# High and low parts in place of plain 32-bit matmuls: the convolution norm's two sums and the pointwise projection of stage three

## The chip, the cores and the metric

One Trainium2 chip, one of its cores. The metric is the device time of one launch in microseconds (us), median of the runs. The engines named here: TensorE (PE; PEld is its weight load), VectorE (DVE), ScalarE (ACT), GpSimd (POOL), and SyncE (SP), which issues the loads.

## The reference, cut to what matters

Three transformer-like stages on 256 tokens of width 1024, all in float32. Each stage is a mixer (attention) followed by a gated MLP. The change lies in the third stage's mixer. Beside an attention of 8 heads it has a convolution branch and a pooling branch, and all three are concatenated before the output projection:

```
def layer_norm(x, g, b):
    mu = jnp.mean(xf, axis=-1, keepdims=True)
    var = jnp.mean(jnp.square(xf - mu), axis=-1, keepdims=True)
    y = (xf - mu) * lax.rsqrt(var + EPS)
    return y * g + b

def conformer_conv(u, dw_w, dw_b, ln_g, ln_b, pw_w):   # 256 channels
    a, b = jnp.split(u, 2, axis=-1)
    h = a * jax.nn.sigmoid(b)
    h = causal_depthwise_conv(h, dw_w) + dw_b
    h = layer_norm(h, ln_g, ln_b)
    h = jax.nn.silu(h)
    return h @ pw_w

mix = jnp.concatenate([att, conv, pool], axis=-1)
x = x + mix @ w_out
```

## The kernel before, in words

The channels lie on the partitions and the 256 tokens along the free dimension, so an activation of 1024 channels is eight tiles of 128x256. Weights are streamed from memory in chunks of up to 128x1024 through a ring of six buffers. Every projection is computed from high and low parts: ScalarE copies a chunk to the format `float32r` (`w_hi`, L415, "split high"), VectorE subtracts that from the chunk (`w_lo`, L423, "split low"), and TensorE adds three products, high x high, low x high and high x low. Such a matmul takes one instruction record of TensorE. A matmul on plain float32 operands is recorded as two.

Each engine has its own instruction queue, written out by hand, and works through it in order; an instruction that waits for a semaphore holds up everything behind it in that queue. The order is given by Python functions, one for each engine and stage. In the third stage's mixer they are `att_c_pe`, `att_c_act` and `att_c_dve`. All three loop over n = 0 to 15, the 16 chunks of the q, k, v weights: four head pairs p, four chunks each (o = n mod 4). At each n TensorE runs the 12 matmuls of chunk n (L714 to L716, 384 columns each, 392 for the first pair), ScalarE first splits chunk n+4 high, and VectorE first splits chunk n+3 low. The other steps are hung onto values of n. In the list below, "pair 0" is the first head pair.

- Attention chain of pair p, over about two pairs of chunks: squares (L1024) and v (L1049 to L1052) on ScalarE at the next pair's o = 0; sums (L1188) on VectorE; logarithm and exponential (L1035, L1038) on ScalarE at o = 1; normalised q and k (L1202) on VectorE; transposes (L793) on TensorE at o = 3; q and k copies (L1124, L1217); scores (L860, L806) on TensorE; mask and row maximum (L1262, L1269) on VectorE; exponential `exp_act` (L1132) on ScalarE; division (L1274, L1278) on VectorE; transposes of the probabilities `prob_t_pe` (L949) on TensorE; their copy `prob_t_act` (L1139) on ScalarE. The scores of pair p+1 go to the same PSUM banks as those transposes, so `score_c_pe` waits for `prob_t_act` of pair p (semaphore `aC_ptr`).
- Forget gates of the heads, between them: L1146, L1151 to L1175, and `decay_pe` (L831) after chunk 8, which `decay_act` (L839) on ScalarE waits for ahead of its v copies.
- Convolution branch: depthwise convolution `conv_pe` (L2157) after chunks 1 and 2; its sum over taps and over the two channel tiles on VectorE (L2184, L2187); `ln_sum_pe` (L2191), a matmul with an all-ones matrix that adds over the channels, after chunk 3; centring and squaring on VectorE (L2196 to L2202); `ln_var_pe` (L2206) after chunk 4; reciprocal root on ScalarE (L2210, L2213) at n = 5; scaling (L2218) on VectorE and `ln_silu_act` on ScalarE at n = 6: it loads the table with Silu (L2221), runs two Silu (L2224), and loads the table with logarithm and exponential back (L2226); the pointwise projection `pw_pe` (L2257) after chunk 13; its high and low parts for the output projection at n = 14 (L2263, L2268).
- Pooling branch: a matmul after chunk 5 (L2234), parts at n = 6 (L2242, L2248).

After the loop the output projection (L1363 to L1365) runs with the last pairs' steps between its matmuls, then the MLP.

Of the kernel before, what the change touches and what calls it, by code (L numbers as in the profile page):

```python
# [197 lines left out]
def build(nc, x_d, xa_d, stream_d, par_d, con_d, taps_d, out_d):  # L198
# [10 lines left out]
    def sem(name):  # L209
# [61 lines left out]
    decay_rows = sb("decay_rows", [P, 3 * P], F32R)  # L271
    fg_all = sb("fg_all", [P, 2, 2, 2, LO_ROW], F32R)
    fg_hi, fg_lo = [fg_all[:, n, :, :, 0:HEADS_C] for n in range(2)]
    cv_shift = [[cv_s0[:, c * W_SHIFT:(c + 1) * W_SHIFT] for c in range(SHIFTS)],
                [v_tok[c][:, TOK:TOK + W_SHIFT] for c in range(3)] + [prob_t[:, 0, 2, 0:W_SHIFT]]]
    W_PL = POOL_PAD + TOK
# [112 lines left out]
    ln_dve = sem("ln_dve")  # L389
    ln_act = sem("ln_act")  # L390
    side_lo = sem("side_lo")
    pool_pe = sem("pool_pe")
    pool_hi = sem("pool_hi")

# [1285 lines left out]
    def att_c_pe(eng):  # L1680
        for n in range(N_C):
            p, o = divmod(n, UCH)
            unit_chunk_pe(eng, 2, n)
            if n == 1:
                conv_pe(eng, 0)
            if n == 2:
                conv_pe(eng, 1)
            if n == 3:
                ln_sum_pe(eng)
            if n == 4:  # L1690
                ln_var_pe(eng)
            if o == 0 and p >= 3:
                prob_t_pe(eng, 2, p - 3, 0)
            if o == 1 and p >= 2:
                score_c_pe(eng, p - 2)
            if o == 1 and p >= 3:
                pv_pe(eng, 2, p - 3)
            if n == 5:
                pool_mm_pe(eng)
            if n == 8:  # L1700
                decay_pe(eng)
            if n == N_C - 3:
                pw_pe(eng)
            if o == 3 and p >= 1:
                if p == 1:
                    eng.wait_ge(side_lo, 2)
                if p == 3:
                    eng.wait_ge(side_lo, 4)
                qkt_pe(eng, 2, p - 1)
        p = PAIRS_C - 1  # L1710
        out_first(eng, 2, 0, UPPER)
        prob_t_pe(eng, 2, p - 2, 0)
        out_first(eng, 2, 1, UPPER)
        score_c_pe(eng, p - 1)
        pv_quarters_pe(eng, 2, p - 2)
# [12 lines left out]
        out_first(eng, 2, 5, LOWER)  # L1728
        pv_quarters_pe(eng, 2, p)
        out_first(eng, 2, 6, LOWER)  # L1730
        out_second(eng, 2, 4, UPPER)
        out_first(eng, 2, 7, LOWER)
        out_second(eng, 2, 5, UPPER)
        out_second(eng, 2, 6, UPPER)
        out_second(eng, 2, 7, UPPER)

    def att_c_act(eng):
        for n in range(N_C):
            p, o = divmod(n, UCH)
            split_hi(eng, C_QKV + n + AHEAD_HI)  # L1740
            if o == 0 and p >= 1:
                square_act(eng, 2, p - 1, TOK)
                if p == 1:
                    forget_raw_act(eng)
                if n == 8:
                    decay_act(eng)
                v_act(eng, 2, p - 1)
            if o == 0 and p >= 3:
                prob_t_act(eng, 2, p - 3, 0)
            if n == 5:  # L1750
                ln_rsqrt_act(eng)
            if n == 7:
                forget_hi_act(eng)
            if o == 1 and p >= 1:
                norm_act(eng, 2, p - 1, 0, 4)
            if n == 6:
                pool_mix_act(eng)
                forget_log_act(eng)
                ln_silu_act(eng)
            if o == 2 and p >= 3:  # L1760
                mix_act(eng, 2, p - 3)
            if n == N_C - 2:
                conv_mix_act(eng)
            if o == 2 and p >= 2:
                exp_act(eng, 2, p - 2, 0)
                exp_act(eng, 2, p - 2, 1)
            if o == 3 and p >= 1:
                q_act(eng, 2, p - 1)
        p = PAIRS_C - 1
        square_act(eng, 2, p, TOK)  # L1770
        v_act(eng, 2, p)
        prob_t_act(eng, 2, p - 2, 0)
        norm_act(eng, 2, p, 0, 4)
        split_hi(eng, C_OUT + 4)
        exp_act(eng, 2, p - 1, 0)
        exp_act(eng, 2, p - 1, 1)
        mix_sum_act(eng, 2, p - 2)
        split_hi(eng, C_OUT + 5)
        q_act(eng, 2, p)
        prob_t_act(eng, 2, p - 1, 0)  # L1780
        split_hi(eng, C_OUT + 6)
        exp_act(eng, 2, p, 0)
        exp_act(eng, 2, p, 1)
        mix_sum_act(eng, 2, p - 1)
        split_hi(eng, C_OUT + 7)
        split_hi(eng, C_FFN)
        prob_t_act(eng, 2, p, 0)
        mix_sum_act(eng, 2, p)
        split_hi(eng, C_FFN + 1)
        split_hi(eng, C_FFN + 2)  # L1790
        end_act(eng, 5)
        split_hi(eng, C_FFN + 3)

    def att_c_dve(eng):
        for n in range(N_C):
# [14 lines left out]
            if n == 8:  # L1810
                decay_dve(eng)
            if n == 4:
                ln_center_dve(eng)
            if o == 0 and p >= 1:
                sums_dve(eng, 2, p - 1, 0, 4)
            if o == 1 and p >= 1:
                norm_dve(eng, 2, p - 1, p - 1, 0, 0, 4)
                if p == 1:
                    forget_bias_dve(eng)
            if n == 6:  # L1820
                ln_scale_dve(eng)
                pool_mix_dve(eng)
            if o == 1 and p >= 2:
                mask_dve(eng, 2, p - 2, 0)
            if o == 2 and p >= 3:
# [218 lines left out]
    def pre_act_f(eng):  # L2044

        for n in range(N_PRE):
            split_hi(eng, C_PRE + n + AHEAD_HI)
            if n == 2:
                rows_act(eng, 4)
                cols_act(eng, 2)  # L2050
                nc.scalar.activation(tri[:], con[:, CON_TRI:CON_TRI + 3 * P], ACT.Copy).then_inc(tri_in, 1)
            if n in (3, 5):
                t = n // 2 - 1
# [127 lines left out]
    def conv_out_dve(eng, t):  # L2181
# [3 lines left out]
        if t == 1:  # L2185
            eng.wait_ge(conv_acc, 2)
            nc.vector.tensor_tensor(cv_e[0], cv_acc[0], cv_acc[1], ALU.add).then_inc(conv_acc, 1)  # L2187

    def ln_sum_pe(eng):
        eng.wait_ge(conv_acc, 3)  # L2190
        nc.tensor.matmul(bank(LN_BANK), con[:, CON_ONES:CON_ONES + P], cv_e[0], start=True, stop=True).then_inc(ln_pe, 1)  # L2191

    def ln_center_dve(eng):
        eng.wait_ge(ln_pe, 1)
# [7 lines left out]
        nc.vector.tensor_tensor(cv_e[0], cv_e[0], cv_e[1], ALU.add).then_inc(ln_sq, 1)  # L2202

    def ln_var_pe(eng):
        eng.wait_ge(ln_sq, 3)
        nc.tensor.matmul(bank(LN_BANK, TOK), con[:, CON_ONES:CON_ONES + P], cv_e[0], start=True, stop=True).then_inc(ln_pe, 1)  # L2206

    def ln_rsqrt_act(eng):
        eng.wait_ge(ln_pe, 2)
# [40 lines left out]

    def pw_pe(eng):
        eng.wait_ge(att[2].qe, 2)
        eng.wait_ge(ln_act, 4)
        for o in range(2):
            for t in range(2):
                w = PAR_PW + t * 2 * P + o * P
                last = nc.tensor.matmul(bank(PW_BANK, o * TOK), par[:, w:w + P], cv_a[t], start=(t == 0), stop=(t == 1))  # L2257
        last.then_inc(ln_pe, 1)

    def conv_mix_act(eng):  # L2260
# [327 lines left out]
```

## Time and profile before

| | |
|---|---|
| Time, median of 3 runs | 1024.39 us (1024.37 to 1024.44) |
| Profiled execution, first to last instruction (span) | 1023.2 us |
| What lies around the span | 1.2 us (1024.39 less 1023.2) |
| TensorE busy | 1018.9 us, 8026 matmul records |
| VectorE / ScalarE / GpSimd busy | 880.5 / 687.1 / 349.1 us |
| Granted TensorE clock | 1.000 of full |
| Third stage's mixer, chunks 0 to 15 of q, k, v | about 760.3 to 810.0 us of the span |

The profiled execution has no separate device time in the profile; its span is what the table gives. The ends of matmuls are modelled and overlap (a record of 256 columns lasts 0.28 us where the next one starts 0.11 us later), so for TensorE the starts of the records tell what an operation costs, and its waits show best in the weight loads (PEld). The same holds on ScalarE and VectorE to a lesser degree: the next instruction starts some 0.08 to 0.1 us before the record of the one ahead ends, if it does not need its result.

### The profile page before, as it was taken

Reading aid. Unit: us, or ns where it says so; the run is one execution under the profiler, and the core shown is the slowest. Engines: PE = TensorE matmul, PEld = TensorE weight load, DVE = VectorE, ACT = ScalarE, POOL = GpSimd, SP = SyncE. Lnnn points to the kernel's source line nnn. Section 1 sums busy time; section 2 is a strip of 40 time slices with the busy share of each in tenths; the row PEclk is TensorE's granted clock in tenths of the full one; section 3 lists DMA queues with packets and bytes.
Section 4 is the critical chain, followed back from the end, with each engine's and each line's share of the span. In section 5 each row is a group of like instructions: output and inputs, shape, how many; then the busy total and the mean of one; then the engine's idle time right before and its main releaser. Section 6 shows DMA issues by size and latency. Waiting matters only on the chain.

```text
span 1023.2 us, 22239 instructions
## 1 busy us (share of the span) xinstructions
PE 1018.9 (100%) x8026; PEld 960.4 (94%) x8026; DVE 880.5 (86%) x1535; ACT 687.1 (67%) x1267; POOL 349.1 (34%) x370
## 2 busy tenths in 40 slices
PE   9999999999999999999999999999999999999998
PEld 9999999999999999999999999999998999999998
DVE  7977778787799988887888999988897879999886
ACT  7776766766766665677786766656697776665663
POOL 5312221112255533342111556433350025654332
PEclk9999999999999999999999999999999999999999
DMA  9744465556476666526364566666544536666651
GB/s 318 256 152 151 144 186 155 159 175 205 149 236 195 219 188 202 170 94 217 126 192 153 185 206 213 199 194 193 157 123 135 166 125 213 219 206 195 196 163 42
DMA packets 57753, 183.40 MB, mean 179 GB/s; under 512 B 6352, under 2 KB 9680, under 8 KB 57424
## 3 DMA queue, kind: packets, MB, share of 16 engines
q1 hardware_dynamic: 56816, 181.52, 55.8%
q8 instruction: 45, 0.74, 0.3%
q10 hardware_dynamic: 864, 0.92, 0.3%
q14 instruction: 28, 0.23, 0.1%
HBM read 181.36 MB, written 1.05 MB: 178 GB/s over the span
## 4 chain that ended last, share of the span: by engine, by line
PE 99%; DMA 0%; DVE 0%; ACT 0%; DVEq 0%; issue 0%
PE ps L455 23%; PE ps L457 12%; PE ps L714 10%; PE ps L716 10%; PE ps L715 9%; PE ps L1902 6%; PE ps L1903 6%; PE ps L1904 6%; PE ps L1363 2%; PE ps L1365 2%; PE ps L1364 2%; PE ps L640 1%; PE ps L911 1%; PE ps L806 1%; PE ps L949 1%; PE ps L894 1%
## 5 line engine op out<-in xcount | busy, mean ns | idle before, releaser
L423 DVE TENSOR_TENSOR w_lo<-w_raw,w_hi 128x1024 fp32r<-128x1024 f32 (+2 forms) x369 | 441.2, 1213 | 31.9 <-ACT w_hi L415 31.5
L415 ACT ACTIVATE w_hi<-w_raw 128x1024 fp32r<-128x1024 f32 (+2 forms) x369 | 353.5, 972 | 121.7 <-PE ps L457 102.4
L455 PE MATMUL ps<-xg,w_hi 128*128 128x512 f32 x1056 | 362.8, 390 | 0.0
L457 PE MATMUL ps<-xg,w_lo 128*128 128x256 f32 x1056 | 291.5, 276 | 0.0
L455 PEld LDWEIGHTS ps<-xg,w_hi 128*128 128x128 f32 x1056 | 198.2, 188 | 38.7
L2027 POOL TENSOR_TENSOR prob_t<-prob_t,qkT 128x256 f32<-128x256 f32 x63 | 111.1, 1763 | 257.2 <-ACT prob_t L1948 257.2
L457 PEld LDWEIGHTS ps<-xg,w_lo 128*128 128x128 f32 x1056 | 198.2, 188 | 0.1
L714 PE MATMUL ps<-w_hi,xg 128*128 128x384 f32 (+1 forms) x556 | 192.5, 346 | 0.0
L716 PE MATMUL ps<-w_hi,xg 128*128 128x384 f32 (+1 forms) x556 | 187.3, 337 | 0.0
L715 PE MATMUL ps<-w_lo,xg 128*128 128x384 f32 (+1 forms) x556 | 185.7, 334 | 0.0
L1902 PE MATMUL ps<-g_hi,w_hi 128*128 128x256 f32 x528 | 146.0, 276 | 0.0
L1903 PE MATMUL ps<-g_lo,w_hi 128*128 128x256 f32 x528 | 145.9, 276 | 0.0
L1904 PE MATMUL ps<-g_hi,w_lo 128*128 128x256 f32 x528 | 145.8, 276 | 0.0
L2021 POOL TENSOR_TENSOR qkT<-prob,rms_r 128x256 f32<-128x256 f32 x132 | 122.9, 951 | 16.9 <-DVE prob L1962 12.0
L1995 DVE SCALAR_TENSOR_TENSOR qkT<-qkT,par 128x255 f32<-128x255 f32 (+1 forms) x264 | 112.2, 477 | 6.5 <-ACT qkT L1941 6.4
L1941 ACT ACTIVATE qkT<-qkT,par 128x256 f32<-128x256 f32 x132 | 78.0, 598 | 46.2 <-POOL qkT L2021 44.7
L714 PEld LDWEIGHTS ps<-w_hi,xg 128*128 128x128 f32 x556 | 104.2, 187 | 2.7 <-issue 1.7
L716 PEld LDWEIGHTS ps<-w_hi,xg 128*128 128x128 f32 x556 | 104.5, 188 | 0.0
L715 PEld LDWEIGHTS ps<-w_lo,xg 128*128 128x128 f32 x556 | 104.3, 188 | 0.1
L1902 PEld LDWEIGHTS ps<-g_hi,w_hi 128*128 128x128 f32 x528 | 99.1, 188 | 2.6 <-issue 0.2
L1904 PEld LDWEIGHTS ps<-g_hi,w_lo 128*128 128x128 f32 x528 | 99.1, 188 | 0.0
L1903 PEld LDWEIGHTS ps<-g_lo,w_hi 128*128 128x128 f32 x528 | 99.1, 188 | 0.0
(196 smaller groups left out, 1382.0 us busy)
## 6 DMA issues: line engine op xcount, KB each, us to landing
w_raw<-w_stream SPq DMA_DIRECT2D x228, 512.0 KB, 3.8
w_raw<-w_stream SPq DMA_DIRECT2D x137, 384.0 KB, 3.6
w_raw<-w_stream SPq DMA_DIRECT2D x4, 392.0 KB, 3.1
con<-consts SPq DMA_DIRECT2D x1, 1024.0 KB, 6.8
x_all<-x_t SPq DMA_DIRECT2D x4, 256.0 KB, 5.1
conv_taps<-taps SPq DMA_DIRECT2D x1, 1024.0 KB, 7.2
w_raw<-w_stream SPq DMA_DIRECT2D x4, 192.0 KB, 4.5
x_all<-x_a SPq DMA_DIRECT2D x3, 256.0 KB, 5.6
```

Source lines behind the costliest of these rows:

```text
L415: nc.scalar.activation(w_hi[s][:, 0:w], w_raw[s][:, 0:w], ACT.Copy).then_inc(w_hi_done, 1)
L423: nc.vector.tensor_tensor(w_lo(c)[:, 0:w], w_raw[s][:, 0:w], w_hi[s][:, 0:w].bitcast(F32), ALU.subtract).then_inc(w_lo_done, 1)
L455: nc.tensor.matmul(bank(b, 0, 2 * TOK), w_hi[s][:, k * P:(k + 1) * P], xg[:, k, :, :].rearrange("p h t -> p (h t)"), start=(k == 0), stop= ...
L457: last = nc.tensor.matmul(bank(b), w_lo(c)[:, k * P:(k + 1) * P], xg_hi[:, k, :], start=False, stop=(k == KT - 1), skip_group_check=True)
L714: nc.tensor.matmul(out, hi, wh, start=(k == 0), stop=False)
L715: nc.tensor.matmul(out, hi, wl, start=False, stop=False)
L716: last = nc.tensor.matmul(out, lo, wh, start=False, stop=(k == KT - 1))
L1902: nc.tensor.matmul(acc(m), wh, g_hi[b][:], start=first, stop=False, skip_group_check=True)
L1903: nc.tensor.matmul(acc(m), wh, g_lo[b][:], start=False, stop=False, skip_group_check=True)
L1904: last = nc.tensor.matmul(acc(m), wl, g_hi[b][:], start=False, stop=True, skip_group_check=True)
L1995: nc.vector.scalar_tensor_tensor(cv_s[b][s][:, k:TOK], up_s[b][s][:, 0:TOK - k], par_col(f, t, per, i, 4 * s + 2 - k), cv_s[b][s][:, k:TOK ...
L2021: nc.gpsimd.tensor_tensor(up_s[t % 2][s], up_sum[s], rms_r[:], ALU.mult).then_inc(F.up, 1)
```

## The change

The two sums over channels and the pointwise projection no longer use plain float32 operands. Their inputs are split into a `float32r` high part (a copy on ScalarE) and a low part (a subtraction on VectorE), in tiles of `mix_hi` and `mix_lo` that are free until the mixer's results come. The all-ones matrix needs no low part, so each sum is two matmuls; the projection is three matmuls for each of its four old ones. The steps are hung onto later values of n: the sum after chunk 4 (was 3), the variance after chunk 6 (was 4), the Silu with its table loads at n = 9 (was 6), and the scaling on VectorE at n = 8 (was 6).

```
+    ones_r = sb("ones_r", [P, P], F32R)
+    ln_hi, ln_lo = mix_hi[:, 2, :], mix_lo[:, 2, :]
+    pw_hi, pw_lo = [m[:, 0:2, :].rearrange("p k t -> p (k t)") for m in (mix_hi, mix_lo)]
+    silu_hi, silu_lo = mix_hi[:, 2:4, :], mix_lo[:, 2:4, :]
...
 att_c_pe:
-            if n == 3:
+            if n == 4:
                 ln_sum_pe(eng)
-            if n == 4:
+            if n == 6:
                 ln_var_pe(eng)
...
 att_c_act:
-            if n == 5:
-                ln_rsqrt_act(eng)
+            if n == 4:
+                ln_part_act(eng, LN_SUM)
+            if n == 6:
+                ln_part_act(eng, LN_VAR)
...
             if n == 6:
                 pool_mix_act(eng)
                 forget_log_act(eng)
+            if n == 7:
+                ln_rsqrt_act(eng)
+                pw_part_act(eng)
+            if n == 9:
                 ln_silu_act(eng)
+                silu_part_act(eng)
+            if n == N_C - 2:
+                conv_mix_act(eng)
             if o == 2 and p >= 3:
                 mix_act(eng, 2, p - 3)
-            if n == N_C - 2:
-                conv_mix_act(eng)
...
 att_c_dve:
             if n == 4:
+                ln_part_dve(eng, LN_SUM)
+            if n == 5:
                 ln_center_dve(eng)
+            if n == 6:
+                ln_part_dve(eng, LN_VAR)
+            if n == 10:
+                silu_part_dve(eng)
...
             if n == 6:
+                pool_mix_dve(eng)
+            if n == 8:
+                pw_part_dve(eng)
                 ln_scale_dve(eng)
-                pool_mix_dve(eng)
...
 pre_act_f, at n == 2:
+                nc.scalar.activation(ones_r[:], con[:, CON_ONES:CON_ONES + P], ACT.Copy)
...
+    def ln_part_act(eng, no):
+        if no == LN_SUM:
+            eng.wait_ge(conv_acc, 3)
+        else:
+            eng.wait_ge(ln_sq, 3)
+        nc.scalar.activation(ln_hi, cv_e[0], ACT.Copy).then_inc(part_hi, 1)
+
+    def ln_part_dve(eng, no):
+        eng.wait_ge(part_hi, PART0 + no)
+        nc.vector.tensor_tensor(ln_lo, cv_e[0], ln_hi.bitcast(F32), ALU.subtract).then_inc(part_lo, 1)
+
+    def ln_rows_pe(eng, no, out):
+        eng.wait_ge(tri_in, 1)
+        eng.wait_ge(part_lo, PART0 + no)
+        nc.tensor.matmul(out, ones_r[:], ln_hi, start=True, stop=False)
+        nc.tensor.matmul(out, ones_r[:], ln_lo, start=False, stop=True).then_inc(ln_pe, 1)
...
+    def silu_part_act(eng):
+        eng.wait_ge(ln_act, 4)
+        for t in range(2):
+            last = nc.scalar.activation(silu_hi[:, t, :], cv_a[t], ACT.Copy)
+        last.then_inc(part_hi, 1)
...
 pw_pe:
-        eng.wait_ge(ln_act, 4)
+        eng.wait_ge(part_lo, PART0 + SILU)
...
-                last = nc.tensor.matmul(bank(PW_BANK, o * TOK), par[:, w:w + P], cv_a[t], start=(t == 0), stop=(t == 1))
+                nc.tensor.matmul(bank(PW_BANK, o * TOK), pw_hi[:, w:w + P], silu_hi[:, t, :], start=(t == 0), stop=False)
+                nc.tensor.matmul(bank(PW_BANK, o * TOK), pw_hi[:, w:w + P], silu_lo[:, t, :], start=False, stop=False)
+                last = nc.tensor.matmul(bank(PW_BANK, o * TOK), pw_lo[:, w:w + P], silu_hi[:, t, :], start=False, stop=(t == 1))
```

`pw_part_act`, `pw_part_dve` and `silu_part_dve` are the same copy and subtraction for the projection's weights (128x512) and for the low part of the Silu's output (two tiles of 128x256).

Three places show what moves. The first is ScalarE's queue after the v copies of pair 0 (L1052), before the change; L415 is the split of chunk 9, L2210 and L2213 the norm's reciprocal root, L1035 and L1038 the attention's:

```order
L1052 ACTIVATE v_tok<-ps,r_c 128x128 [waits tiles]
L415 ACTIVATE w_hi<-w_raw 128x768 [waits tiles,w_loaded3]
L2210 ACTIVATE ln_x<-ps,con 128x256 [waits ln_pe]
L2213 ACTIVATE ln_x<-ln_x 128x256 [waits ln_act]
L1035 ACTIVATE ln_q<-ss_q,con,r_c 128x4 [waits aC_ss,c_r2]
```

The same place now, where L1058, L421 and L1041 are the old L1052, L415 and L1035, and L2217 is the new high part:

```order
L1058 ACTIVATE v_tok<-ps,r_c 128x128 [waits tiles]
L2217 ACTIVATE mix_hi<-qkT 128x256 [waits conv_acc]
L421 ACTIVATE w_hi<-w_raw 128x768 [waits tiles,w_loaded3]
L1041 ACTIVATE ln_q<-ss_q,con,r_c 128x4 [waits aC_ss,c_r2]
L1041 ACTIVATE ln_q<-ss_q,con,r_c 128x4 [waits aC_ss]
```

The high part of the sum's input stands behind the v copies, which themselves come after chunk 3; the root has gone from here. The second place is TensorE between the last matmuls of chunk 3 and the first of chunk 5, before the change (the ones left out are the 12 of chunk 4):

```order
L716 MATMUL ps<-w_hi,xg 128x392
L2191 MATMUL ps<-qkT,con 128x256 [waits conv_acc]
L714 MATMUL ps<-w_hi,xg 128x384 [waits pre_out,w_lo_done]
...
L716 MATMUL ps<-w_hi,xg 128x384
L2206 MATMUL ps<-qkT,con 128x256 [waits ln_sq]
L714 MATMUL ps<-w_hi,xg 128x384 [waits w_lo_done]
```

And now, with L720 and L722 for L714 and L716, from the end of chunk 3 to the start of chunk 5 (`half_lo` is the semaphore of the low parts):

```order
L722 MATMUL ps<-w_hi,xg 128x392
L720 MATMUL ps<-w_hi,xg 128x384 [waits pre_out,w_lo_done]
...
L722 MATMUL ps<-w_hi,xg 128x384
L2226 MATMUL ps<-mix_hi,ones_r 128x256 [waits half_lo,tri_in]
L2227 MATMUL ps<-mix_lo,ones_r 128x256
L720 MATMUL ps<-w_hi,xg 128x384 [waits w_lo_done]
```

The sum now stands a chunk later, and it waits for VectorE's low part. The third place is ScalarE between the logarithm of pair 1 (n = 9) and the exponential of pair 0 (n = 10), before:

```order
L1035 ACTIVATE ln_q<-ss_q,con,r_c 128x4 [waits aC_ss]
L1038 ACTIVATE r_q<-ln_q 128x8 [waits aC_ln]
L415 ACTIVATE w_hi<-w_raw 128x768 [waits tiles,w_loaded2]
L1132 ACTIVATE prob,ssum<-prob,nmax 128x128 [waits aC_nmax]
L1132 ACTIVATE prob,ssum<-prob,nmax 128x256
```

and now, where L2278 and L2283 are the table loads, L2281 the Silu, L2242 the new high parts, and L1138 the exponential:

```order
L1044 ACTIVATE r_q<-ln_q 128x8 [waits aC_ln]
L2278 ACT_TABLE_LOAD
L2281 ACTIVATE qkT<-qkT,par 128x256 [waits ln_dve] x2
L2283 ACT_TABLE_LOAD
L2242 ACTIVATE mix_hi<-qkT 128x256 [waits ln_act]
L2242 ACTIVATE mix_hi<-qkT 128x256
L421 ACTIVATE w_hi<-w_raw 128x768 [waits tiles,w_loaded2]
L1138 ACTIVATE prob,ssum<-prob,nmax 128x128 [waits aC_nmax]
```

The loads and the Silu now stand ahead of the exponential of pair 0, with the two new copies behind them.

## Rows read from the trace of the kernel before

**Rows 1.** The page: span, and busy time of each engine.

```profile
span 1023.2 us, 22239 instructions
PE 1018.9 (100%) x8026; PEld 960.4 (94%) x8026; DVE 880.5 (86%) x1535; ACT 687.1 (67%) x1267; POOL 349.1 (34%) x370
```

**Rows 2.** Waits of the weight loads, 740 to 1023 us: total, times, longest.

```profile
PEld ps L2206 <- DVE qkT L2202: 0.2, 1, 0.2
```

**Rows 3.** Timeline of PE around the two sums: start, duration, instruction, idle before.

```profile
775.45 0.34 PE L716 MATMUL ps<-w_hi,xg 128*128 128x392 f32 x1
775.63 0.59 PE L2191 MATMUL ps<-qkT,con 128*128 128x256 f32 x2
...
776.24 0.34 PE L715 MATMUL ps<-w_lo,xg 128*128 128x384 f32 x1
...
777.98 0.34 PE L716 MATMUL ps<-w_hi,xg 128*128 128x384 f32 x1
778.20 0.70 PE L2206 MATMUL ps<-qkT,con 128*128 128x256 f32 x2
...
778.91 0.33 PE L715 MATMUL ps<-w_lo,xg 128*128 128x384 f32 x1
```

**Rows 4.** Timeline of PE around the pointwise projection.

```profile
802.08 0.51 PE L860 MATMUL ps<-decay_rows,head_row 128*128 128x384 f32 x2
...
804.03 1.99 PE L2257 MATMUL ps<-qkT,par 128*128 128x256 f32 x8
...
806.04 0.34 PE L715 MATMUL ps<-w_lo,xg 128*128 128x384 f32 x1
```

**Rows 5.** Timeline of PE in the projections ahead: three matmuls of 256 columns.

```profile
754.90 0.28 PE L441 MATMUL ps<-xg,w_hi 128*128 128x256 f32 x1
...
755.24 0.28 PE L441 MATMUL ps<-xg,w_hi 128*128 128x256 f32 x1
```

**Rows 6.** Timeline of ACT after chunk 3.

```profile
777.32 0.37 ACT L1052 ACTIVATE v_tok<-ps,r_c 128x128 f32<-128x128 f32 x1
777.59 0.84 ACT L415 ACTIVATE w_hi<-w_raw 128x768 fp32r<-128x768 f32 x1
```

**Rows 7.** Timeline of ACT: an operation of 256 columns, and the next.

```profile
835.80 0.40 ACT L515 ACTIVATE tokbuf<-x_all 128x256 f32<-128x256 f32 x1
836.11 0.49 ACT L509 ACTIVATE xg<-x_all,par 128x256 fp32r<-128x256 f32 x1
```

**Rows 8.** Timeline of DVE: an operation of 256 columns, and the next.

```profile
777.72 0.42 DVE L2202 TENSOR_TENSOR qkT<-qkT 128x256 f32<-128x256 f32 x1
778.06 0.74 DVE L1188 TENSOR_REDUCE ss_q<-tokbuf 128x4 f32<-128x256 f32 x2
```

**Rows 9.** Timeline of ACT: the Silu and its table loads.

```profile
783.03 0.22 ACT L1161 ACTIVATE fg<-fg 128x16 f32<-128x16 f32 x1
783.26 1.28 ACT L2221 ACT_TABLE_LOAD   x1
784.56 1.10 ACT L2224 ACTIVATE qkT<-qkT,par 128x256 f32<-128x256 f32 x2
785.67 1.28 ACT L2226 ACT_TABLE_LOAD   x1
786.97 0.85 ACT L415 ACTIVATE w_hi<-w_raw 128x768 fp32r<-128x768 f32 x1
```

**Rows 10.** Timeline of ACT from the logarithm of pair 1 to `prob_t_act`.

```profile
792.40 0.21 ACT L1038 ACTIVATE r_q<-ln_q 128x8 f32<-128x8 f32 x1
792.51 0.83 ACT L415 ACTIVATE w_hi<-w_raw 128x768 fp32r<-128x768 f32 x1
794.86 0.40 ACT L1132 ACTIVATE prob<-prob,nmax 128x128 f32<-128x128 f32 x1 [1.52 <-DVE nmax L1269]
...
800.38 0.81 ACT L1139 ACTIVATE prob_t<-ps 128x768 f32<-128x768 f32 x1
```

**Rows 11.** Timeline of PE: the decay matmuls, and the transposes of pair 0's probabilities.

```profile
788.74 0.65 PE L831 MATMUL ps<-tri,fg_all 128*40 128x384 f32 x6
...
799.35 0.82 PE L949 MATMUL ps<-con,prob 128*128 128x128 f32 x6
```

**Rows 12.** Timeline of ACT: waits for TensorE behind the projection.

```profile
806.06 0.66 ACT L2263 ACTIVATE mix_hi<-ps 128x256 fp32r<-128x256 f32 x2 [1.53 <-PE ps L2257]
810.66 0.39 ACT L1124 ACTIVATE qkT<-ps 128x256 f32<-128x256 f32 x1 [1.25 <-PE ps L793]
```

More of the change, by code:

```diff
@@ L391, in build @@
     side_lo = sem("side_lo")
+    part_hi, part_lo, PART0 = half_hi, half_lo, HALVES
+    LN_SUM, LN_VAR, PW_W, SILU = 1, 2, 3, 4
     pool_pe = sem("pool_pe")
@@ L2187, in conv_out_dve, with pw_part_act, pw_part_dve, silu_part_dve @@
             nc.vector.tensor_tensor(cv_e[0], cv_acc[0], cv_acc[1], ALU.add).then_inc(conv_acc, 1)
-    def ln_sum_pe(eng):
-        eng.wait_ge(conv_acc, 3)
-        nc.tensor.matmul(bank(LN_BANK), con[:, CON_ONES:CON_ONES + P], cv_e[0], start=True, stop=True).then_inc(ln_pe, 1)
+    def ln_part_act(eng, no):
[12 more added lines that the diff above has]
+        nc.tensor.matmul(out, ones_r[:], ln_lo, start=False, stop=True).then_inc(ln_pe, 1)
+    def ln_sum_pe(eng):
+        ln_rows_pe(eng, LN_SUM, bank(LN_BANK))
+    def pw_part_act(eng):
+        nc.scalar.activation(pw_hi, par[:, PAR_PW:PAR_PW + 4 * P], ACT.Copy).then_inc(part_hi, 1)
+    def pw_part_dve(eng):
+        eng.wait_ge(part_hi, PART0 + PW_W)
+        nc.vector.tensor_tensor(pw_lo, par[:, PAR_PW:PAR_PW + 4 * P], pw_hi.bitcast(F32), ALU.subtract).then_inc(part_lo, 1)
+    def silu_part_act(eng):
[3 more added lines that the diff above has]
+        last.then_inc(part_hi, 1)
+    def silu_part_dve(eng):
+        eng.wait_ge(part_hi, PART0 + SILU)
+        for t in range(2):
+            last = nc.vector.tensor_tensor(silu_lo[:, t, :], cv_a[t], silu_hi[:, t, :].bitcast(F32), ALU.subtract)
+        last.then_inc(part_lo, 1)
     def ln_center_dve(eng):
@@ L2204, in ln_var_pe @@
     def ln_var_pe(eng):
-        eng.wait_ge(ln_sq, 3)
-        nc.tensor.matmul(bank(LN_BANK, TOK), con[:, CON_ONES:CON_ONES + P], cv_e[0], start=True, stop=True).then_inc(ln_pe, 1)
+        ln_rows_pe(eng, LN_VAR, bank(LN_BANK, TOK))
     def ln_rsqrt_act(eng):
@@ L2252, in pw_pe @@
         eng.wait_ge(att[2].qe, 2)
-        eng.wait_ge(ln_act, 4)
+        eng.wait_ge(part_lo, PART0 + SILU)
         for o in range(2):
             for t in range(2):
-                w = PAR_PW + t * 2 * P + o * P
-                last = nc.tensor.matmul(bank(PW_BANK, o * TOK), par[:, w:w + P], cv_a[t], start=(t == 0), stop=(t == 1))
+                w = t * 2 * P + o * P
+                nc.tensor.matmul(bank(PW_BANK, o * TOK), pw_hi[:, w:w + P], silu_hi[:, t, :], start=(t == 0), stop=False)
+                nc.tensor.matmul(bank(PW_BANK, o * TOK), pw_hi[:, w:w + P], silu_lo[:, t, :], start=False, stop=False)
+                last = nc.tensor.matmul(bank(PW_BANK, o * TOK), pw_lo[:, w:w + P], silu_hi[:, t, :], start=False, stop=(t == 1))
         last.then_inc(ln_pe, 1)
```

## The prediction

> **What bounds the kernel now.** I read the page first: TensorE is busy for 1018.9 of 1023.2 us [rows 1]. Then the waits of its weight loads, because the ends of its matmuls are modelled: from 740 us to the end there is one wait for another engine, 0.2 us at the variance matmul, for VectorE [rows 2]. So TensorE's queue is the time. Work taken out of it is a gain at once, and every new wait in it is a loss at once, with nothing behind it to give it back. The reader has to keep two sums apart: what the matmuls cost by the distance of their starts, and when ScalarE and VectorE are ready for the waits that now stand at other places. For those I read the timelines of the three engines from 775 to 811 us.
>
> **The matmuls.** From the last L716 of chunk 3 to the L715 of chunk 4 are 0.79 us (775.45 to 776.24), around one plain 32-bit matmul [rows 3]. Ten steps later, 777.98 less 776.24, gives 0.174 us for each of the projection's matmuls, so two steps without the sum would be 0.35, and the sum costs 0.44. The same around the variance: 778.91 less 777.98 is 0.93, less 0.35 is 0.58, of which 0.10 is the restart after its wait (778.20 to 778.91 is 0.71, against 0.61 from 775.63 to 776.24 without a wait) and some 0.04 the wait. The four matmuls of the pointwise projection and the change back take 2.01 us, 804.03 to 806.04 [rows 4].
> The new ones have the shape and the format of L441 to L443: three of them in 0.34 us, so 0.114 each [rows 5]. Each sum becomes 2 x 0.114 = 0.23, the projection 12 x 0.114 + 0.17 = 1.54. TensorE's own work falls by 0.21 + 0.35 + 0.47 = 1.03 us. I take the format's price as certain to 0.1 us: reading the parts from the mixer's tiles is what the output projection does too.
>
> **The first new wait: the sum after chunk 4.** Its high part stands on ScalarE behind the v copies. Those end at a time that the change does not touch: L1052 starts at 777.32 and the next instruction at 777.59 [rows 6]. The copy takes 0.40 us [rows 7], to 777.99. VectorE has been free since its split and answers 0.04 later, 0.42 for the subtraction [rows 8], to 778.45; TensorE's weight load follows 0.06 after such an end (777.72 + 0.42 = 778.14 to 778.20 [rows 3, 8]), and with the restart of 0.10 the first matmul counts from 778.61. TensorE, without the old sum, ends chunk 4 at 775.63 + 12 x 0.174 = 777.72. The wait is 0.89 us. What waits behind it is all of TensorE's queue. On VectorE the subtraction stands ahead of pair 0's sums and of the split of chunk 8, which TensorE needs four chunks later.
> The variance follows the same way: centring comes after the split on VectorE, some 1.9 us of it, and the low part is ready at about 784.1, where TensorE ends chunk 6 at about 784.2. I count it as hidden, by 0.1 us; if the cover is gone it costs what it is late, plus 0.16 of restart. Together to this point: 0.89 + 0.23 + 0.23 - 0.44 - 0.58 = +0.33 us.
>
> **The second: Silu and table loads in front of the exponential of pair 0.** `decay_pe` starts 0.33 later than 788.74 [rows 11], and ScalarE, which waits for it, is late by the same. Without Silu at n = 6 it reaches that wait early, and the time saved there is lost in waiting for TensorE. At n = 9 the block goes in behind L1038: the load starts when that is over (783.03 + 0.22 against 783.26 [rows 9]), 0.11 later than the next instruction does now; then from load to load 2.41 (783.26 to 785.67), 1.30 for the second load, and two copies of 0.31 each (835.80 to 836.11 [rows 7]): 0.11 + 2.41 + 1.30 + 0.62 = 4.44 us. Against it stands the idle time that ScalarE has ahead of the exponential: it could begin at 792.51 + 0.74 (the distance of such a split is the 0.83 of its record less 0.09) = 793.25 and begins at 794.86 [rows 10], 1.61 us. So the exponential is late by 0.33 + 4.44 - 1.61 = 3.16.
> From there to `prob_t_act` of pair 0, at 800.38, ScalarE has no idle time now [rows 10], so the 3.16 arrive there whole. The scores of pair 1 wait for that copy: it now ends at 801.19, with 0.06 + 0.10 of restart 801.35, and TensorE comes at 802.08 [rows 4]. The slack is 0.73. TensorE will start those scores 3.16 - 0.73 = 2.43 us late. The transposes at L949, 799.35 [rows 11], wait first, by about 1.1 us, since the division needs the exponential; this is inside the 2.43 and not added to it, and so is the 0.33 of before.
> The projection then gives its 0.47 back: +1.96 at chunk 14. After it ScalarE has two waits for TensorE now, 1.53 and 1.25 us [rows 12], in which its remaining lateness over TensorE (3.16 against 1.96, and 0.3 for the mix copy that now stands behind the projection's) is gone. From there everything moves by the same amount to the end.
>
> **Edits that I cost at nothing.** The copy of the ones (128x128, at about 753 us), the high and low parts of the projection's weights (128x512) and the scaling at n = 8 stand where ScalarE or VectorE wait for TensorE soon after. The Silu needs the scaling, which I put 1.7 us before it; that is the cover, and each us beyond it would be one of time. No DMA is added or moved; SP's queue waits for low splits that are needed some ten us later.
>
> **A rule against rows.** The loads last 1.28 us, and the Silu starts 1.30 after the load does [rows 9]. The Trainium skill, "ScalarE: Activation LUTs", section "What ACT_TABLE_LOAD costs", puts a drain of about 1.38 us beside the load, about 2.66 us for a switch. By that rule two switches would cost some 2.7 us more than the rows show, and the sum would be near 1029; the rows here hold no such drain but for the 0.11 above, and I go by them.
>
> **The sum.** -1.03 (matmuls) + 0.89 (first wait) + 2.10 (the waits at the transposes and scores, 2.43 less 0.33) = +1.96 us. The profiled span would go from 1023.2 to 1025.1, and with the 1.2 us around it the time from 1024.39 to 1026.3. What a measurement here can tell from no change is 0.2%, 2.05 us. The forecast lies just inside.
> The spread of its terms: restart of TensorE 0.06 to 0.25 in place of 0.16, twice; copies on ScalarE 0.31 to 0.40; how much of the 0.33 reaches ScalarE, 0 to 0.33; slack 0.5 to 0.9. Together 1025.6 to 1027.0.
>
> **Rivals.**
> 1. The Silu block is absorbed. ScalarE gets 3.7 us freed at n = 6, and if it carried that forward, the exponential would be in time. Then only the first wait counts: +0.33 - 0.47 = -0.14, 1024.2. For it: the total of work hardly grows. Against it: ScalarE must wait for `decay_pe` in between, so it can't be early after 789 us.
> 2. All waits hidden, the plain gain: -1.03, 1023.4. It needs the low part of the sum before 777.66. Against it: the v copies alone end later.
> 3. Slower than can be overlooked: the Silu waits for VectorE's scaling. There the subtraction of 128x512 and the scaling come behind the decay's low part and pair 1's sums. It decides once VectorE is more than 1.7 us later than I put it; a further split's worth (some 0.9 us) beyond that gives +2.9, 1027.3. For it: VectorE waits for ScalarE's decay copy first. Against it: I find nothing to fill the 1.7.
> 4. The drain of the rule above is real at this place: +4.7, 1029.1.
> 5. The format doesn't give one pass here: 16 matmuls at the old price of about 0.43 instead of 0.114 would be some +5, 1031. Against it: all projections of this kernel, same kind of tiles.
>
> **How the numbers follow.** Forecast 0.70; rival 1: 0.12; rival 2: 0.05; rival 3: 0.10; rivals 4 and 5: 0.03 together. Over 0.2% slower starts at 1026.44: of the forecast's own 0.70 I put 0.28 above it and 0.42 below, with rivals 3 to 5 that is 0.41 slower. Faster by over 0.2% would be under 1022.34, beyond even rival 2: 0.01. Rest 0.58. The predicted time is the forecast's, 1026.3. The range leaves out rival 2, half of rival 1 and the top: 1024.4 to 1027.4; the forecast's own is 1025.6 to 1027.0.
>
> **What would show it.** In the profile after: the waits of TensorE's weight loads list three new ones, at the first sum for VectorE (about 0.8 us), at the transposes of pair 0 for VectorE (about 1.1), at the scores of pair 1 for ScalarE (about 1); each of the new matmuls starts 0.11 us after the one ahead; the exponential of pair 0 starts near 798 with no idle time before it; and from chunk 14 on all starts lie 1.9 to 2.0 us later. The prediction is wrong if TensorE reaches the scores of pair 1 without waiting, if the variance waits for more than 0.3 us, if a Silu waits for VectorE, or if the lateness of chunk 14 is not that of the end.

## The result, and the profile after

| | before | after |
| --- | --- | --- |
| Median of 11 runs | 1024.44 us (1024.20 to 1024.73) | 1027.03 us (1026.55 to 1027.65) |
| Ratio to before | | 1.0026, 95% interval 1.0018 to 1.0034 |
| Span of the profiled run | 1023.2 us | 1025.1 us |

The changed kernel is slower by 2.6 us, 0.26%; forecast were +1.9 us, range 1024.4 to 1027.4. The median falls on the slower side of the bound of 0.2% that the forecast stood just inside of, but the interval reaches from 0.18% to 0.34% and so holds that bound.

The page after, span and busy times, against [rows 1]:

```profile
span 1025.1 us, 22260 instructions
PE 1018.4 (99%) x8030; PEld 958.7 (94%) x8030; DVE 881.8 (86%) x1540; ACT 688.9 (67%) x1273; POOL 348.7 (34%) x370
```

TensorE's busy time falls by 0.5 us while the span grows by 1.9: the time went into waits. The span of before is of one execution that was long in its first part: in every run that has both figures the time is 1.8 us more than the span (1.76 to 1.88), so a time of 1024.4 goes with a span of 1022.6, and the typical span grew by 2.6. The weight loads' waits after, 740 us to the end (total, times, longest), against [rows 2]:

```profile
PEld ps L955 <- DVE prob L1284: 1.2, 1, 1.2
PEld ps L2226 <- issue: 1.0, 1, 1.0
PEld ps L866 <- ACT prob_t L1145: 0.9, 1, 0.9
...
PEld ps L1923 <- issue: 0.3, 1, 0.3
...
PEld ps L2314 <- issue: 0.2, 1, 0.2
```

Three are at the places forecast: the transposes of pair 0 (L955, before L949), the first sum (L2226), the scores of pair 1 (L866, before L860). The second says "issue", but PE's own timeline names the releaser, the low part's subtraction L2221:

```profile
778.21 0.35 PE L2226 MATMUL ps<-mix_hi,ones_r 128*128 128x256 f32 x1 [0.72 <-DVE mix_lo L2221]
778.40 0.28 PE L2227 MATMUL ps<-mix_lo,ones_r 128*128 128x256 f32 x1
...
783.91 0.28 PE L2226 MATMUL ps<-mix_hi,ones_r 128*128 128x256 f32 x1
784.03 0.28 PE L2227 MATMUL ps<-mix_lo,ones_r 128*128 128x256 f32 x1
...
800.39 0.87 PE L955 MATMUL ps<-con,prob 128*128 128x128 f32 x6 [0.87 <-DVE prob L1284]
...
803.94 0.61 PE L866 MATMUL ps<-decay_rows,head_row 128*128 128x384 f32 x2 [0.59 <-ACT prob_t L1145]
...
805.99 0.39 PE L2314 MATMUL ps<-mix_hi 128*128 128x256 f32 x1
806.21 0.28 PE L2315 MATMUL ps<-mix_lo,mix_hi 128*128 128x256 f32 x1
806.33 0.28 PE L2316 MATMUL ps<-mix_hi,mix_lo 128*128 128x256 f32 x1
...
807.53 0.34 PE L720 MATMUL ps<-w_hi,xg 128*128 128x384 f32 x1
807.71 0.34 PE L721 MATMUL ps<-w_lo,xg 128*128 128x384 f32 x1
```

Rows 3, 4 and 11 of before have their counterparts here. The variance (783.91) has no wait, as forecast. ScalarE's timeline shows the block of the Silus behind the logarithm of pair 1, against [rows 9, 10]:

```profile
789.45 0.48 ACT L845 ACTIVATE decay_rows<-ps 40x384 fp32r<-40x384 f32 x1 [0.91 <-PE ps L837]
...
792.41 0.21 ACT L1044 ACTIVATE r_q<-ln_q 128x8 f32<-128x8 f32 x1
792.63 1.28 ACT L2278 ACT_TABLE_LOAD   x1
793.93 1.09 ACT L2281 ACTIVATE qkT<-qkT,par 128x256 f32<-128x256 f32 x2
795.04 1.28 ACT L2283 ACT_TABLE_LOAD   x1
796.33 0.72 ACT L2242 ACTIVATE mix_hi<-qkT 128x256 fp32r<-128x256 f32 x2
796.96 0.83 ACT L421 ACTIVATE w_hi<-w_raw 128x768 fp32r<-128x768 f32 x1
797.70 0.38 ACT L1138 ACTIVATE prob<-prob,nmax 128x128 f32<-128x128 f32 x1
...
803.08 0.80 ACT L1145 ACTIVATE prob_t<-ps 128x768 f32<-128x768 f32 x1
```

The exponential starts at 797.70 with no idle time before it; it was 794.86 after 1.52 of idle time. The copy that the scores wait for starts at 803.08 in place of 800.38.

**How two traces are laid on each other.** Executions differ by some tenths at the first loads and between 741 and 755 us, whatever the kernel. So each instruction of TensorE was matched with the same one of before, and the difference of their starts is given relative to that at 755 us, ahead of everything in dispute but the copy of the ones (752.75 in the changed kernel). That copy shows no cost: between 741 and 755 us the kernels fall into two groups, about 0.37 us apart, and both groups hold kernels with it and without it (after and before; after_again and order_only). Columns are times in the trace of before (us); 779 is behind the two sums of before, 799.5 the transposes, 802.3 the scores, 806.1 behind the projection, 1016 and 1019 the last MLP.

| Kernel | 779.0 | 784.5 | 799.5 | 802.3 | 806.1 | 1016 | 1019 |
| --- | --- | --- | --- | --- | --- | --- | --- |
| after | +0.16 | +0.38 | +1.47 | +2.33 | +2.04 | +1.90 | +2.32 |
| after_again | +0.17 | +0.38 | +1.48 | +2.34 | +2.05 | +2.06 | +2.48 |
| order_only | -0.60 | -0.17 | +0.31 | +1.18 | +1.18 | +1.03 | +1.09 |
| pw_only | 0.00 | 0.00 | 0.00 | 0.00 | -0.29 | -0.43 | -0.37 |
| sum_early | -0.79 | -0.56 | +0.53 | +1.39 | +1.09 | +0.95 | +1.37 |
| no_tables | +0.16 | +0.38 | +0.51 | +0.52 | +0.23 | +0.23 | +0.65 |
| copies_twice | +0.16 | +0.38 | +2.08 | +2.94 | +2.64 | +2.49 | +2.90 |
| refit | -0.79 | -0.45 | -0.45 | -0.45 | -0.74 | -0.87 | -0.46 |
| refit_pad | -0.79 | -0.44 | -0.43 | -0.43 | -0.72 | -0.86 | -0.80 |
| pad_five | 0.00 | 0.00 | -0.01 | -0.01 | -0.01 | -0.19 | +0.14 |
| before_pad, pad_act | 0.00 | 0.00 | 0.00 to -0.01 | 0.00 to -0.01 | 0.00 to -0.01 | -0.01 to -0.03 | +0.06 to +0.04 |

What was open after the result: whether the waits come from the order, the table loads or the format; why the projection gave 0.29 instead of 0.47; and where the 0.42 us between 1016 and 1019 come from, which no step had.

### The profile page after: what moved, and what is told of

Its sections match the earlier page's. It is cut to its first block, busy times and chain, and to the rows that moved or that the text cites. A ratio compares the mean times of both kernels' runs of the same rounds, so it can differ in the third digit from the quotient of the medians.

```text
span 1025.1 us, 22260 instructions
## 1 busy us (share of the span) xinstructions
PE 1018.4 (99%) x8030; PEld 958.7 (94%) x8030; DVE 881.8 (86%) x1540; ACT 688.9 (67%) x1273; POOL 348.7 (34%) x370
## 4 chain that ended last, share of the span: by engine, by line
PE 97%; ACT 1%; issue 1%; DVE 1%; DMA 0%; POOLq 0%; POOL 0%; DVEq 0%; ACTq 0%
PE ps L461 23%; PE ps L463 12%; PE ps L720 9%; PE ps L722 9%; PE ps L721 9%; PE ps L1923 6%; PE ps L1925 6%; PE ps L1924 6%; PE ps L1369 2%; PE ps L1371 2%; PE ps L1370 2%; PE ps L646 1%; PE ps L917 1%; PE ps L812 1%; PE ps L955 1%
## 5 line engine op out<-in xcount | busy, mean ns | idle before, releaser
L421 ACT ACTIVATE w_hi<-w_raw 128x1024 fp32r<-128x1024 f32 (+2 forms) x369 | 353.6, 972 | 121.2 <-PE ps L463 102.5
L720 PE MATMUL ps<-w_hi,xg 128*128 128x384 f32 (+1 forms) x556 | 192.0, 345 | 0.1
L722 PE MATMUL ps<-w_hi,xg 128*128 128x384 f32 (+1 forms) x556 | 187.3, 337 | 0.0
L720 PEld LDWEIGHTS ps<-w_hi,xg 128*128 128x128 f32 x556 | 104.3, 188 | 2.8 <-issue 1.9
L722 PEld LDWEIGHTS ps<-w_hi,xg 128*128 128x128 f32 x556 | 104.5, 188 | 0.0
```

What stands on the lines that cost most here:

```text
L421: nc.scalar.activation(w_hi[s][:, 0:w], w_raw[s][:, 0:w], ACT.Copy).then_inc(w_hi_done, 1)
L720: nc.tensor.matmul(out, hi, wh, start=(k == 0), stop=False)
L722: last = nc.tensor.matmul(out, lo, wh, start=False, stop=(k == KT - 1))
```

## The experiments

**order_only: the order alone.** The changed kernel's order with the plain operands and without any part; in short:

```diff
-            if n == 4:
-                ln_part_act(eng, LN_SUM)
...
-                silu_part_act(eng)
...
-        ln_rows_pe(eng, LN_SUM, bank(LN_BANK))
+        eng.wait_ge(conv_acc, 3)
+        nc.tensor.matmul(bank(LN_BANK), con[:, CON_ONES:CON_ONES + P], cv_e[0], start=True, stop=True).then_inc(ln_pe, 1)
```

> The new places of the steps with the old plain 32-bit operands: no high or low parts at all, sum after chunk 4, variance after chunk 6, Silu with its table loads at n = 9. Theory A (the cost is the place of the Silu block on ScalarE): TensorE waits neither at the sum nor at the variance (-0.14 us), the block without its two copies is 3.82 us, so the exponential of pair 0 is late by 3.82 - 1.61 - 0.14 = 2.07 and the scores of pair 1 by 2.07 - 0.73 = 1.34; time 1.3 to 1.6 us over before, about 1025.9. Theory B (the cost is the parts, their copies and subtractions): within 0.4 us of before, about 1024.5.

Measured: 1025.57 us, ratio 1.0009 (1.0000 to 1.0018); before on this chip 1024.39. In the trace +1.09 at the end. The waits at the transposes and the scores are there without any part:

```profile
PEld ps L866 <- ACT prob_t L1145: 0.9, 1, 0.9
PEld ps L955 <- DVE prob L1284: 0.6, 1, 0.6
```

So moving the Silu block to chunk 9's turn costs 1.35 us (784.5 to 802.3) with the old operands; the first wait and the rest come with the parts. The time is 1.18 over before, a little under the 1.3 to 1.6 expected.

**pw_only: the format at the projection alone.** The kernel before, with the projection's twelve matmuls and its parts taken where ScalarE and VectorE are idle (in short; the weights' low part is taken at n = 7):

```diff
+            if n == 3:
+                pw_part_act(eng)
...
+            if n == 9:
+                silu_part_act(eng)
...
+            if n == 13:
+                silu_part_dve(eng)
```

> The kernel before with its norm and Silu where they were, and only the pointwise projection from high and low parts; the weights' parts and the Silu's parts stand where ScalarE and VectorE are idle (n = 3 and 9, n = 7 and 13). Theory A (the format gains what the spacing of the matmuls says, and only waits cost): the projection takes 1.54 in place of 2.01 us and nothing waits; 0.47 less than before, about 1023.9. Theory B (parts cost more than they give): not faster than before, 1024.4 or more.

Measured: 1024.43 us, ratio 0.9997 (0.9988 to 1.0006): the times can't tell it from before, and the 1023.9 expected of the spacing was not reached. The trace can tell: nothing moves up to 802.3, and behind the projection it is 0.29 ahead, not 0.47, with no wait in it. It is the price of the matmuls that was off, the same in both kernels.

**sum_early: the sum's high part ahead.** The changed kernel with one call moved up on ScalarE, ahead of the squares and v copies:

```diff
             split_hi(eng, C_QKV + n + AHEAD_HI)
+            if n == 4:
+                ln_part_act(eng, LN_SUM)
             if o == 0 and p >= 1:
                 square_act(eng, 2, p - 1, TOK)
```

> The changed kernel with the high part of the sum's input on ScalarE ahead of pair 0's squares and v copies instead of behind them. Theory A (ScalarE is tied to TensorE at the decay copy, so what the first wait costs arrives at the end): the wait of about 0.9 us at the sum is gone, the scores of pair 1 are earlier by the same, 0.9 us less than the changed kernel, about 1026.1. Rival: the scores' start is set by ScalarE's own work alone, the wait at the sum lies inside what is lost later anyway, and the time stays at that of the changed kernel, about 1027.0.

Measured: 1026.04 us, ratio 1.0017 (1.0008 to 1.0026). The first matmul of the sum no longer waits:

```profile
777.45 0.28 PE L2226 MATMUL ps<-mix_hi,ones_r 128*128 128x256 f32 x1
777.56 0.28 PE L2227 MATMUL ps<-mix_lo,ones_r 128*128 128x256 f32 x1
```

At 779 it stands at -0.79 against +0.16, so that the first wait is worth 0.95, and 0.95 of it are still there at the end: this wait in TensorE's queue was not given back.

**no_tables: the block without its loads.** The Silus become a scale and shift (the activation is left out), and both table loads go:

```diff
-        nc.scalar.preload_act_table_set("silu_and_others")
...
-            nc.scalar.activation(cv_a[t], cv_b[t], ACT.Silu, scale=par[:, PAR_LNG + t:PAR_LNG + t + 1],
+            nc.scalar.activation(cv_a[t], cv_b[t], ACT.Identity, scale=par[:, PAR_LNG + t:PAR_LNG + t + 1],
...
-        nc.scalar.preload_act_table_set("natural_log_exp_and_others")
```

> The changed kernel without the two table loads; the Silu is replaced by scale and bias alone, so the activation is left out. Theory A (ScalarE's lateness less the slack of 0.73 us is what TensorE waits): the block shrinks from 4.44 to about 1.73 us, the exponential of pair 0 is late by 0.45 us, under the slack, the waits at the transposes and at the scores vanish and only the first remains: 1024.2 to 1024.5, some 2.5 us under the changed kernel. Rival (lateness is passed on whole, without slack, or the loads are hidden): 1024.7 to 1025.0 if whole, 1027.0 if hidden.

Measured: 1025.11 us, ratio 1.0008 (0.9999 to 1.0017), at least 0.6 us above what the first theory gave and near the rival's 1024.7 to 1025.0. The trace goes against that rival: the waits at the transposes and scores are nearly gone (0.14 between 784.5 and 802.3, where the changed kernel loses 1.95), ScalarE has idle time again,

```profile
795.25 0.40 ACT L1138 ACTIVATE prob<-prob,nmax 128x128 f32<-128x128 f32 x1 [0.59 <-DVE nmax L1275]
```

and the late piece at the end of the last MLP (+0.42 between 1016 and 1019) has stayed. That piece belongs to neither mechanism.

One thing in the expectation was wrong: the exponential is late by 1.19 us (795.25 + 0.80 - 794.86, the 0.80 being this trace's shift at 755), not by 0.45, for it now waits for VectorE's row maximum. (TensorE is only 0.52 late at the scores and does not wait there, so that the slack that the rival denies is there.) The row maximum is late in the changed kernel too; before and after:

```profile
794.66 0.17 DVE L1269 TENSOR_SCALAR nmax<-smax 128x4 f32<-128x4 f32 x1
```

```profile
795.48 0.17 DVE L1275 TENSOR_SCALAR nmax<-smax 128x4 f32<-128x4 f32 x1
```

With the 0.37 of that trace it is 1.19 late. Part of it goes with TensorE's own lateness: in sum_early, where TensorE is 0.94 us earlier, it is 0.25 late. For the rest VectorE has the weights' low part (L2237) and the scaling (L2275) ahead of it. In the changed kernel ScalarE's 3.21 covers this.

**copies_twice: 0.6 us more in the block.** Two more copies behind the Silus:

```diff
+            nc.scalar.activation(silu_lo[:, t, :], cv_a[t], ACT.Copy)
+        for t in range(2):
             last = nc.scalar.activation(silu_hi[:, t, :], cv_a[t], ACT.Copy)
```

> The changed kernel with two more 128x256 copies on ScalarE (0.30 to 0.31 us each) behind the Silus, ahead of the copies of the parts. Theory A (the block of the Silus is on the path one for one, through the exponential of pair 0, the transposes and the scores): +0.6 us over the changed kernel, about 1027.6. Rival (the wait at the scores has another cause, such as VectorE's probabilities): within 0.1 us of the changed kernel, 1027.0.

**after_again: the changed kernel again, beside it.**

> The changed kernel itself, unaltered, beside the others on the same chip: 1027.0 us. Both theories expect the same of it; the trace tells whether the 0.45 us wait of VectorE at the end of the last MLP (between the end of ScalarE's copy and the addition behind it) comes again in another execution. If it belongs to the code, it is there; if to one execution, it need not be.

Measured: copies_twice 1027.53 us (ratio 1.0031, 1.0020 to 1.0043), after_again 1026.84 us (1.0022, 1.0012 to 1.0031); before beside them 1024.47. The block grows by 0.62, and the wait at the transposes from 0.87 to

```profile
800.57 0.87 PE L955 MATMUL ps<-con,prob 128*128 128x128 f32 x6 [1.48 <-DVE prob L1284]
```

0.61 more; at the scores +2.94 against +2.34. One for one, as the theory says. The late piece came again in both.

**refit: the same format at other places.** The sum's part as in sum_early; the weights' parts in chunks 3 and 7; the variance behind the pool's matmuls of chunk 5 (before: after chunk 4) and the reciprocal root at n = 6 (before: 5); the Silu block at n = 6, where the kernel before has it; the Silus' parts in chunks 9 and 13. In short:

```diff
             if n == 5:
                 pool_mm_pe(eng)
+                ln_var_pe(eng)
...
                 pool_mix_act(eng)
+                ln_rsqrt_act(eng)
                 forget_log_act(eng)
+                ln_silu_act(eng)
```

> All three edits of operands as in the changed kernel, at other places: the sum's high copy ahead of the squares (as in sum_early), the variance and its high part back behind the pool's matmuls of chunk 5, the logarithm and the Silu block with its two table loads back in chunk 6's turn, the weights' parts taken in chunks 3 and 7, the Silus' parts in chunks 9 and 13. Theory A (the time went to where the copies and the table loads stand, not to the format): no new wait of TensorE before the projection, so the matmuls' savings are all kept: 0.21 + 0.35 + the 0.28 that the projection gave in the trace after = 0.84 us less than before, 1023.6; with the 0.33 us that came at the end of the last MLP in every kernel with the changed kernel's instructions, 1023.9. Rival (the format itself is dear in this place, by its copies on two busy engines): at or above before, 1024.4 or more, with waits at the transposes and scores of pair 0.

Measured: 1024.38 us, ratio 0.9996 (0.9987 to 1.0006): not to be told from before, and at the rival's 1024.4 rather than at the 1023.9 expected. The trace has none of the waits that the rival needs, and behind the projection it is 0.74 ahead, of the 0.84 expected. The 0.10 that are missing lie at the variance, which costs 0.34 at its new place (-0.79 to -0.45) where it cost 0.23 in the changed kernel; its weight load has no releaser in the profile:

```profile
PEld ps L2224 <- issue: 0.5, 1, 0.5
```

At 1016 it is 0.87 ahead. The 0.13 between come in pw_only, order_only, sum_early and even pad_five as well (0.14 to 0.18) and are no part of the edit. Then it loses 0.41 in the last MLP.

**before_pad, pad_five, pad_act, refit_pad: the late piece.** The timeline of VectorE in the last MLP after, and of ScalarE ahead of it (the changed kernel):

```profile
1017.31 0.43 DVE L2027 TENSOR_TENSOR prob_t<-prob_t,qkT 128x256 f32<-128x256 f32 x1 [0.45 <-ACT prob_t L1969]
```

```profile
1016.50 0.42 ACT L1969 ACTIVATE prob_t<-qkT 128x256 f32<-128x256 f32 x1 [0.95 <-DVE qkT L2016]
```

ScalarE ends at 1016.92 and VectorE starts 0.39 later; before the change it starts at once. This stood in after, after_again, sum_early, no_tables, copies_twice and refit, and not in before, order_only and pw_only. All six with it have five instructions more on VectorE, the other three none or three. The test is to add empty instructions at the start, where the engines wait for the first data (ScalarE's are six ACTIVATE of 128x2):

```diff
             nc.vector.memset(zero[:], 0.0).then_inc(warm, 1)
+            for n in range(6):
+                nc.vector.memset(cv_s0[:, 2 * n:2 * n + 2], 0.0)
```

> The kernel before with six memsets of 128x2 on VectorE at the very start, where it waits 3 us for the first data; they leave its stream of instructions about as long as the changed kernel's. Theory (the 0.33 us at the end of the last MLP comes from where VectorE's code stands, not from what it computes): in the trace VectorE's last multiply-add of the last MLP starts 0.4 us after ScalarE's copy instead of 0.04, and the time is 0.3 us over before, 1024.7. Rival (it comes from the parts' work or from TensorE's or ScalarE's code): no such gap, 1024.4.

> The kernel before with five, not six, memsets of 128x2 on VectorE at its start: its stream is then exactly as long as in the changed kernel, in sum_early, no_tables and refit (2405 records), all of which show the late addition in the last MLP. Theory P (it hangs on where exactly VectorE's code stands, and six moved it past): the last addition of the last MLP starts 0.4 us after ScalarE's copy ends, and TensorE's last matmuls come 0.33 us later than in the kernel before. Rival (the position of TensorE's or ScalarE's code, or the parts themselves): 0.04 us, as with six.

> The kernel before with six ACTIVATE of 128x2 on ScalarE at its start, in its wait for the first data: its stream is as long as in the changed kernel (2143 records). Theory P (VectorE's code alone decides): 0.04 us between ScalarE's copy and VectorE's addition in the last MLP. Rival Q (ScalarE's code decides): 0.4 us there, and TensorE's end 0.33 us later.

> refit with one memset of 128x2 on VectorE at its start. Theory P: VectorE's code is moved by one more instruction, as with six before, so the late addition of the last MLP goes and TensorE's last matmuls come 0.33 us earlier than in refit: its trace ends 0.85 us before the kernel before when both are set even at 70 us, about 1023.6 to 1024.0. Rival: the addition is still 0.4 us late, and the time is that of refit, 1024.4.

Measured: before_pad (six) 1024.70 us, ratio 0.9998 (0.9989 to 1.0007); pad_five 1024.57 us and pad_act 1024.38 us in one run each; refit_pad 1023.77 us, ratio 0.9991 (0.9982 to 1.0000), before 1024.41. VectorE's addition in before_pad, in pad_five, and in refit_pad:

```profile
1015.08 0.43 DVE L2006 TENSOR_TENSOR prob_t<-prob_t,qkT 128x256 f32<-128x256 f32 x1
```

```profile
1014.97 0.42 DVE L2006 TENSOR_TENSOR prob_t<-prob_t,qkT 128x256 f32<-128x256 f32 x1 [0.45 <-ACT prob_t L1948]
```

```profile
1014.53 0.42 DVE L2025 TENSOR_TENSOR prob_t<-prob_t,qkT 128x256 f32<-128x256 f32 x1
```

With five memsets the kernel before has the wait, with six it has not, and with six on ScalarE it has not; one memset more takes it out of refit. The times can't decide this: before_pad lies at the 1024.7 that its theory expected, and yet has no wait in its trace. It went against the theory only because it was made with six. The place of VectorE's code, not its work, decides in these runs, and it decides to the instruction; pad_five and pad_act have one run and one trace each. One row goes along with it. The queue that the profile calls "q14 instruction" brings one last packet of 8 KB, and six instructions more on VectorE move it from 1016.91 to 1010.02 (6.5 us, counted from the common point), six on ScalarE by 0.3. In the seven kernels with the late piece it starts 0.67 to 0.90 us behind the addition, in before, order_only, pw_only and pad_act 1.20 to 1.47 behind it, and in before_pad and refit_pad 5 us ahead. So the wait comes where this transfer lies closest behind the addition; that the addition waits for code is not shown, and the cause stays open.

## Why the prediction came out so

By its own steps, each in us on TensorE:

| Step | forecast | measured |
| --- | --- | --- |
| Sums in parts and first wait, to 784.5 | +0.33 | +0.38 |
| Exponential of pair 0 late, against 794.86 | 3.16 | 3.21 (797.70, less the -0.37 at 755) |
| Waits at transposes and scores | +2.10 | +1.95 |
| Projection | -0.47 | -0.29 |
| From there to 1016 | 0 | -0.14 (0.00 in after_again) |
| Last MLP, 1016 to 1019 | 0 | +0.42 |
| Sum | +1.96 | +2.32 |

- **The two waits: right, in place, cause and size.** The experiments take each away alone: sum_early the first (0.95), no_tables the second (1.81 of 1.95), and copies_twice moves the second one for one. The slack at the scores was forecast as 0.73: ScalarE's copy L1145 is 803.08 - 800.38 + 0.37 = 3.07 late, TensorE 2.33, so it was 0.74. The 3.16 were to "arrive there whole"; of the 3.21 that started out 0.14 were lost on the way (5.52 us from the exponential to the copy before, 5.38 now), and this is most of why the second term came out at 1.95 and not 2.10.
- **What the second is made of.** order_only shows that most of it, 1.35 from 784.5 to 802.3, is the Silu block behind the exponential's turn; the two copies of the parts add 0.60, the rest of the 1.95. The forecast had put both into one block of 4.44 and did not say that the order alone would cost so much.
- **The projection was mis-sized, by 0.18.** The step "12 x 0.114 + 0.17 = 1.54" fails: the matmuls start 0.12 apart, and behind the first there are 0.22, so that twelve take 1.54 (805.99 to 807.53) and with the change back 1.72, against 2.01 [rows 4]. The spacing of [rows 5] was that of another stretch (0.07 over twelve). The other 0.10 belong to the first: its weight load (L2314) has 0.2 of "issue" ahead of it. The 2.01 began with such a start too (the line below, of before), and by taking only the new spacing the sum counted its going as a gain.

```profile
804.03 1.59 PEld L2257 LDWEIGHTS ps<-qkT,par 128*128 128x128 f32 x8 [0.17 <-issue]
```

- **The end of the last MLP was in no step.** "From there everything moves by the same amount to the end" is the sentence that failed. The piece is 0.42, of which 0.06 to 0.07 are in the kernels without the late addition too. The prediction had named this as a sign of being wrong: the lateness of chunk 14, +2.04, is not that of the end, +2.32.
- **The side of the bound.** The medians lie 2.59 apart, in the second measurement 2.37 (1026.84 less 1024.47); the traces explain 2.3 to 2.5. The chances of 0.58 and 0.41 hung on 0.1 us. Without the last MLP the errors of the steps cancel by luck (+0.05, -0.15, +0.18 and -0.14), and the trace would be +1.90, inside the bound of 2.05; the 0.42 took it over.
- **The span: right by luck.** The forecast said 1025.1 and the profile has 1025.1, though the change cost more than the +1.96. The prediction started from the span of 1023.2 and took 1.2 us to lie around it, where all later runs have 1.8; the trace of before is the longest to 755 us of all that were taken, 0.37 longer than that of after. The forecast of the time added +1.96 to 1024.39 and does not hang on it.
- **The edits costed at nothing** did not reach TensorE, but not all were idle time: with the scaling, the weights' low part is in the 1.19 by which VectorE's row maximum is late, and only ScalarE's greater lateness hides it.
- **The rivals.** The absorbed block, the plain gain, the Silu behind VectorE's scaling (L2281 starts with no idle time; the scaling L2275 ends at 792.56 and the Silu starts at 793.93, a cover of 1.37 where 1.7 was forecast) and the old price for the format are all refuted by rows above. So is the drain: the second load starts at 795.04 and the next instruction at 796.33. The Trainium skill, "ScalarE: Activation LUTs", section "What ACT_TABLE_LOAD costs", puts a drain of about 1.38 us beside each load. This trace has none but 0.11 ahead of the first. no_tables, with both loads gone, has its exponential 2.02 us earlier than the changed kernel (relative to 755 us) and 0.59 of idle time ahead of it: together 2.61, the loads' own 2.56 with nothing beside them.

In refit the format was worth 0.74 us behind the projection; the changed kernel is at +2.04 there, so that its placement cost 2.78, almost four times as much. refit_pad, the same arithmetic at other places, is the only version whose time may be called lower than before: 0.64 us under it in the medians, 0.80 in the trace, at the edge of what eleven runs can tell.

## What to carry to other kernels

When one engine's queue is the time, price an edit as two sums: what its own instructions save, and where each producer that it adds or moves stands in the other engines' queues. Here 0.3 us copies behind the wrong neighbours and a block of table loads ahead of an exponential outweighed every matmul saved, and the same format at idle places gave 0.74 of its 0.84. Where effects of 0.3 us matter, compare traces instruction by instruction from a common point, and try a few empty instructions before explaining a residue.

## What the runs showed of the hardware

- One VectorE instruction late in a kernel started 0.39 us after its releaser where five instructions had been added ahead of it in VectorE's code, and 0.03 to 0.04 after it where none, three or six had. At the end of TensorE's queue it was 0.27 to 0.36 us. The last 8 KB packet of an instruction queue moved with it; whether it is the cause is open.
- Plain 32-bit matmuls of 256 columns cost TensorE about 0.44 us by the distance of starts, those in the projections' format 0.114 in one stretch and 0.12 in another.
- Two executions of the changed kernel differ by 0.30 us in the first 70 us and by another 0.36 between 741 and 755, as much as the terms in dispute.
- The time of a launch is 1.8 us (1.76 to 1.88) more than its span in every run that has both.
